# A new opening for a two-block transformer kernel, and its forget-gate logits as split fp32r matmuls

## The chip, the core and the metric

The kernel runs on one core of a Trainium2 chip. The metric is the device time of one execution in microseconds (us); less is better.

## What is computed

Two transformer blocks are applied to one sequence of 256 tokens of width 2048, in fp32. Only the start of the first block is touched by the change:

```
xn = rms_norm(x, norm_mix_g)                  # x: 256 x 2048
proj = xn @ w_in                              # w_in: 2048 x 12296
xa, xpool, xsc, qkv, f_logit, gate_logits = split(proj, ...)
...                                           # xa, xpool, xsc, qkv feed four branches
log_f = log_sigmoid(f_logit + forget_b)       # f_logit: 256 x 8
cum = cumsum(log_f, axis=tokens)              # used in the attention branch
```

The normalization is x * g * rsqrt(mean(x*x) + eps). The kernel multiplies by the gain g (`g_mix`) before the matmul and by the rsqrt factor (`rstd`) after it.

## The kernel before

**Layout.** Activations are held transposed: 16 tiles of 128 channels x 256 tokens. A number is kept as a high part and a low part, both of the type fp32r. `act_a[:, k, 0:S]` is the high part of tile k and `act_a[:, k, S:2*S]` the low part (S = 256).

**Units and pieces.** The weight matrices are read as pieces of 512 rows x 256 columns (512 KB). A unit is 256 output columns, in most phases four pieces (`ppu` = 4, s = 0 to 3). A piece is brought by a transfer that SyncE issues into one of four places of `raw` (L547), copied to fp32r by ScalarE (`w_high`, L879), and the difference is taken by VectorE (`w_low`, L1216). TensorE then does eight pairs of matmuls per piece: high weights by high and low activations in one matmul of 512 columns (L580), and low weights by high activations in one of 256 columns (L582). Semaphores: `raw_full[slot]` (transfer landed), `high_ready`, `split_done` (piece n is split; SyncE waits on it before it refills the place, TensorE before it uses the piece), `w_used` (TensorE has used the piece; ScalarE waits on it before it overwrites `w_high`).

**End of a unit (epilogue).** ScalarE copies the low half of the sums from PSUM (`bcopy`, L893), VectorE adds (`summ`, L1241, semaphore `summed`) and multiplies by `rstd` (L1248). There are two PSUM banks for units, so TensorE starts unit n only when unit n-2 is in `summ`. On ScalarE and VectorE the order is written out: the pieces of the next unit are put ahead of the epilogue of this one (`skewed`).

**Opening.** SyncE issues x as four transfers of four tiles, then all parameter columns (`par`, 249.5 KB), the constants (`common`), and then pieces as their places come free. ScalarE waits for `par`, and for each two tiles of x it makes their squares (`sqt`, L982) and high parts (L984); after every four tiles it casts one piece of the first unit. VectorE makes the low parts (L1343) and w_low of that piece. GpSimd (POOL) adds the squares into `sqacc` (L1657), two tiles at a time, and then starts its own transfers of small operands (L1736 to L1743), among them `w_f`, the eight columns of the forget gate. TensorE works through unit 0 of `proj_a`, piece by piece, then sums the squares over the partitions with a matrix of ones (`ssq`, L615 and L616), and goes on with the other nine units of `proj_a`. From the sum come `rms` (ScalarE, L971) and `rstd` (VectorE, L1332).

**Forget-gate logits.** After the ten units of `proj_a` TensorE computes the logits with fp32 matmuls, 16 tiles by two halves:

```
for k in range(KT):
    for half in range(2):
        last = nc.tensor.matmul(pm[0:HEADS, 0, 0:S], w_f[:, k, :],
                                act_a[:, k, half * S:half * S + S].bitcast(F32), ...)     # L628
```

VectorE takes them from PSUM (L1384, L1385), ScalarE applies abs, exp and ln (L1003 to L1005), VectorE the scan (L1390). Meanwhile TensorE goes on with `proj_b`, three pieces, then the small matmuls of the first branch step (L642, L643, L648). All later phases follow in the same manner.

Of the kernel before, what the change touches and what calls it, by code (L numbers as in the profile page):

```python
# [18 lines left out]
F32 = mybir.dt.float32  # L19
# [5 lines left out]
P = 128  # L25
S = 256
# [92 lines left out]
def plan():  # L119

    ph = [Phase("proj", 10, 2, 4, name="proj_a"), Phase("proj", 6, 2, 4, name="proj_b")]
    for step, q in (("gates", 0), ("gates", 1), ("mix", 0), ("mix", 1),
# [43 lines left out]
def piece_no(ph, i, j, s):  # L166

    return i * (ph.U * ph.ppu) + (ph.piece0 + j * ph.ppu + s)

# [28 lines left out]
def build(nc, A, out):  # L198
# [4 lines left out]
    with ExitStack() as ctx:  # L203
# [22 lines left out]
        rms_buf = sb("rms", [P, S])  # L226
        stat = sb("stat", [P, 84])
        ps = ctx.enter_context(nc.psum_tensor("ps_gemm", [P, 2, 2, 2 * S], F32))
        pm = ctx.enter_context(nc.psum_tensor("ps_small", [P, 4, 2 * S], F32))
# [21 lines left out]
        def pcol(name, i=0):  # L251
# [22 lines left out]
            sem("in_" + n) for n in ("params", "common", "consts1", "w_f", "selectors", "consts2", "p", "resid"))  # L274
        in_x = [sem(f"in_x{b}") for b in range(4)]
        stored = sem("stored")
# [6 lines left out]
        zeroed, bd_zeroed = sem("zeroed"), sem("bd_zeroed")  # L283
        y_high, y_done = sem("y_high"), sem("y_done")
        f_logits, f_biased, f_log, cum_ready, cumt_ps, cumt_ready = (
            sem(n) for n in ("f_logits", "f_biased", "f_log", "cum_ready", "cumt_ps", "cumt_ready"))
# [30 lines left out]
        def source(ph, i, j, s):  # L317
# [3 lines left out]
            k0, kn = 4 * s, 4  # L321
            if n == "proj_a":
                w, c = "w_in", u * 256
            elif n == "proj_b":
                w, c = "w_in", u * 256 + 2560
# [31 lines left out]
        def slot(ph, j, s):  # L357
            return (j * ph.ppu + s) % RING

# [111 lines left out]
        def dst_tile(ph, i, j):  # L471

            q, n, u = ph.quarter, ph.name, i * ph.U + j
            if n == "proj_b":
# [84 lines left out]
        def _(pe):  # L559
# [4 lines left out]

            def piece(ph, x_in, need, i, j, s):

# [6 lines left out]
                pe.wait_ge(split_done, piece_no(ph, i, j, s) + 1 + RING)  # L573
                for k in range(kn):
                    x = x_in(i, j, 4 * s + k)
                    first = s == 0 and k == 0
# [40 lines left out]


            pe.wait_ge(in_common, 16)
# [244 lines left out]
        def _(act):  # L864
# [5 lines left out]
            def piece(ph, i, j, s):  # L870
# [4 lines left out]
                body_rounds = ph.U * ph.ppu // RING  # L875
                rnd = i * body_rounds + (ph.piece0 + j * ph.ppu + s) // RING + 1
                act.wait_ge(raw_full[at], rnd * 16)
# [96 lines left out]
            eps_t = stat[:, 64:65]  # L974

            act.wait_ge(in_par, 16)

            for b in range(8):
                act.wait_ge(in_x[b // 2], 16)
                if b >= 2:  # L980
                    act.wait_ge(sq0_added, b - 1)
                nc.scalar.activation(sqt[:, b % 2], tiles(G, 2 * b, 2), ACT.Square).then_inc(sq0_ready, 1)  # L982
                for t in range(2):
                    last = nc.scalar.activation(act_a[:, 2 * b + t, 0:S], G[:, 2 * b + t, :], ACT.Copy,  # L984
                                                scale=pcol("g_mix", 2 * b + t))
                last.then_inc(hi0, 1)
                if b % 2:
                    piece(BY["proj_a"], 0, 0, b // 2)
            act.wait_ge(zeroed, 1)
# [215 lines left out]
        def _(dve):  # L1205
# [21 lines left out]
            def epilogue(ph, i, j):  # L1227
# [14 lines left out]
                if k in ("proj", "gate", "up", "upconv"):  # L1242
                    dve.wait_ge(summed, n + 1 + 2)
                    r2 = rstd[:].unsqueeze(1).to_broadcast([P, 2, S])
                    if k == "proj":
                        dst = proj_tiles(ph, t0)
                        dve.wait_ge(epi_done, n + 2)
                        nc.vector.tensor_tensor(dst, s2, r2, ALU.mult).then_inc(epi_done, 1)  # L1248
                        return
# [87 lines left out]
            nc.vector.memset(stat[:, 64:65], EPS).then_inc(zeroed, 1)  # L1337
            dve.wait_ge(in_par, 16)
            for b in range(8):
                dve.wait_ge(hi0, b + 1)  # L1340
                for t in range(2):
                    k = 2 * b + t
                    last = nc.vector.scalar_tensor_tensor(out=act_a[:, k, S:2 * S], in0=G[:, k, :],  # L1343
                                                          scalar=pcol("g_mix", k), in1=act_a[:, k, 0:S].bitcast(F32),
                                                          op0=ALU.mult, op1=ALU.subtract)
                last.then_inc(lo0, 1)
                if b % 2:
                    piece(BY["proj_a"], 0, 0, b // 2)

# [15 lines left out]

            pend = skewed(dve, None, BY["proj_a"], pieces, epilogue, True, once=lambda: recip(0))
            ended = []
# [280 lines left out]
        def _(pool):  # L1648
# [191 lines left out]
```

## Time and profile before

| | |
|---|---|
| median of 3 runs | 3088.48 us (3086.43 to 3089.05) |
| the profiled execution's own time | 3071.16 us |
| its span | 3069.3 us |
| mean granted TensorE clock | 0.988 |
| TensorE (PE) busy | 2967.5 us, 97% |
| VectorE (DVE) busy | 1973.4 us, 64% |
| ScalarE (ACT) busy | 1551.1 us, 51% |
| GpSimd (POOL) busy | 257.8 us, 8% |

Times in rows of the trace are counted from the start of the span. An engine's busy time is the time in which at least one of its instructions ran. PEld is the load of stationary operands, which overlaps matmuls. The idle time before an instruction is put down to what released it last.

### The profile page before, as it was taken

The numbers are of one execution on the slowest core, as the hardware profiler recorded it, in microseconds if no ns is written. First come the engines' busy times: TensorE is split into PE (matmuls) and PEld (weight loads), VectorE is DVE, ScalarE is ACT, GpSimd is POOL, SyncE is SP. The second block draws the span as 40 slices with busy tenths as digits, with TensorE's granted clock in tenths as the row PEclk, the third lists the DMA queues.
The fourth block names the chain that finished last, engine by engine and source line by source line (L and its number), as shares of the span: only waits on it lengthen the run. The fifth ranks groups of instructions, "written<-read, shape, count | busy, mean of one in ns | idle before, by whom it ended". The sixth has DMA issues, their size and how long they took to land. (4 is left out here: it accounts for less than half of the span.)

```text
span 3069.3 us, 48743 instructions
## 1 busy us (share of the span) xinstructions
PE 2967.5 (97%) x16830; PEld 2571.2 (84%) x16830; DVE 1973.4 (64%) x2245; ACT 1551.1 (51%) x1953; POOL 257.8 (8%) x217
## 2 busy tenths in 40 slices
PE   7999999999999999999999998999799999999979
PEld 6788888888888888888888887878588888888867
DVE  6486676656665656556656655665777567657664
ACT  5485654454544444444544455444466455545544
POOL 3010011102101010000200000001300000010131
PEclk9999999999999999999999999999899999999989
DMA  7555557665666666665665544546366666565545
GB/s 215 158 165 165 165 167 217 181 178 171 192 192 192 189 188 191 190 187 180 197 191 172 170 148 141 185 151 190 107 187 185 186 190 189 187 185 185 173 134 165
DMA packets 544861, 544.78 MB, mean 177 GB/s; under 512 B 17032, under 2 KB 543880, under 8 KB 544752
## 3 DMA queue, kind: packets, MB, share of 16 engines
q1 hardware_dynamic: 543200, 539.42, 57.7%
q0 software_dynamic: 1552, 3.97, 0.4%
q8 instruction: 60, 0.98, 0.1%
q14 instruction: 49, 0.40, 0.0%
HBM read 541.23 MB, written 2.10 MB: 177 GB/s over the span
## 5 line engine op out<-in xcount | busy, mean ns | idle before, releaser
L1216 DVE TENSOR_TENSOR w_low<-raw,w_high 128x1024 fp32r<-128x1024 f32 x1024 | 1276.3, 1260 | 857.1 <-ACT w_high L879 852.6
L580 PE MATMUL ps_gemm<-act_a,w_high 128*128 128x512 f32 x4640 | 1643.1, 399 | 60.5 <-DVE w_low L1216 39.2
L879 ACT CAST w_high<-raw 128x1024 fp32r<-128x1024 f32 x1024 | 1056.6, 1045 | 961.7 <-PE ps_gemm L582 925.4
L582 PE MATMUL ps_gemm<-act_a,w_low 128*128 128x256 f32 x4640 | 1303.8, 281 | 0.0
L580 PE MATMUL ps_gemm<-act_b,w_high 128*128 128x512 f32 x3520 | 1240.6, 397 | 14.9 <-DVE w_low L1216 5.7
L580 PEld LDWEIGHTS ps_gemm<-act_a,w_high 128*128 128x128 f32 x4640 | 876.9, 189 | 276.6 <-issue 59.5
L582 PE MATMUL ps_gemm<-act_b,w_low 128*128 128x256 f32 x3520 | 986.9, 280 | 0.0
L582 PEld LDWEIGHTS ps_gemm<-act_a,w_low 128*128 128x128 f32 x4640 | 882.6, 190 | 0.2
L580 PEld LDWEIGHTS ps_gemm<-act_b,w_high 128*128 128x128 f32 x3520 | 663.3, 188 | 170.6 <-issue 10.6
L582 PEld LDWEIGHTS ps_gemm<-act_b,w_low 128*128 128x128 f32 x3520 | 667.8, 190 | 0.2
L893 ACT COPY bcopy<-ps_gemm 128x512 f32<-128x512 f32 x300 | 173.6, 579 | 88.1 <-PE ps_gemm L582 88.0
L1241 DVE TENSOR_TENSOR summ<-ps_gemm,bcopy 128x512 f32<-128x512 f32 x276 | 188.8, 684 | 28.1 <-ACT bcopy L893 27.3
L1689 POOL TENSOR_TENSOR proj<-proj,summ 128x512 f32 x32 | 41.4, 1292 | 1016.3 <-DVE summ L1241 1016.3
L1304 DVE SCALAR_TENSOR_TENSOR gates<-summ,params,gates 128x254 f32<-128x254 f32 (+1 forms) x176 | 77.3, 480 | 17.7 <-ACT gates L946 10.7
L1250 DVE TENSOR_TENSOR summ<-summ,rstd 128x512 f32<-128x512 f32 x124 | 85.8, 692 | 4.3
L1675 POOL TENSOR_TENSOR proj<-proj,summ 128x512 f32 x32 | 46.5, 1455 | 400.2 <-DVE summ L1290 400.2
L1657 POOL TENSOR_TENSOR sqacc<-sqacc,sqt 128x512 f32<-128x512 f32 x48 | 67.8, 1413 | 126.4 <-ACT sqt L964 114.3
L912 ACT CAST act_a<-summ 128x512 f32 (+1 forms) x32 | 19.9, 622 | 96.9 <-DVE summ L1263 96.9
L946 ACT ACTIVATE gates<-summ,params 128x256 f32<-128x256 f32 x88 | 48.2, 595 | 21.0 <-DVE summ L1250 19.0
L1257 DVE SCALAR_TENSOR_TENSOR act_b<-proj,params,act_b (+1 forms) x32 | 26.6, 873 | 49.8 <-ACT act_b L905 49.8
L899 ACT ACTIVATE gates<-summ 128x512 f32<-128x512 f32 (+1 forms) x40 | 25.3, 632 | 63.1 <-DVE summ L1250 63.0
L1225 DVE TENSOR_TENSOR act_a<-summ,act_a 128x512 f32 (+1 forms) x32 | 22.2, 693 | 32.5 <-ACT act_a L912 32.5
(239 smaller groups left out, 911.0 us busy)
## 6 DMA issues: line engine op xcount, KB each, us to landing
raw<-in_w_in SPq DMA_DIRECT2D x352, 512.0 KB, 4.2
raw<-in_w_up SPq DMA_DIRECT2D x176, 512.0 KB, 3.6
raw<-in_w_mlp_up SPq DMA_DIRECT2D x128, 512.0 KB, 3.9
raw<-in_w_mlp_down SPq DMA_DIRECT2D x128, 512.0 KB, 4.2
raw<-in_w_down SPq DMA_DIRECT2D x88, 512.0 KB, 4.4
raw<-in_w_out SPq DMA_DIRECT2D x64, 512.0 KB, 4.6
raw<-in_w_branch SPq DMA_DIRECT2D x32, 512.0 KB, 4.0
raw<-in_w_ple_gate SPq DMA_DIRECT2D x32, 512.0 KB, 4.4
```

The lines of the kernel that those rows point to most:

```text
L580: nc.tensor.matmul(ps[:, g, t, :], wh[:, at, o:o + P], x, start=first, stop=False, skip_group_check=True)
L582: last = nc.tensor.matmul(ps[:, g, t, 0:S], wl[:, at, o:o + P], high(x), start=False, stop=final, skip_group_check=True)
L879: nc.scalar.copy(wh[:, at, 0:kn * S], raw[:, at, 0:kn * S]).then_inc(high_ready, 1)
L893: nc.scalar.copy(bcopy[:, g], ps[:, g, :, S:2 * S]).then_inc(b_copied, 1)
L946: last = nc.scalar.activation(G[:, 28 + 2 * j + t, :], summ[:, g, t], ACT.Identity, scale=pcol("conv_w2", c0 + t + 176), bias=pcol("conv_b ...
L1216: nc.vector.tensor_tensor(wl[:, at, 0:kn * S], raw[:, at, 0:kn * S], wh[:, at, 0:kn * S].bitcast(F32), ALU.subtract).then_inc(split_done, 1)
L1241: nc.vector.tensor_tensor(s2, A_half, bcopy[:, g], ALU.add).then_inc(summed, 1)
L1250: nc.vector.tensor_tensor(s2, s2, r2, ALU.mult).then_inc(scaled, 1)
L1304: last = nc.vector.scalar_tensor_tensor(out=y[:, t, sh:S], in0=summ[:, g, t, 0:S - sh], scalar=pcol("conv_w2", c0 + t + 88 * tap), in1=y[: ...
L1657: nc.gpsimd.tensor_tensor(sqacc[:], sqacc[:], sqt[:, g], ALU.add).then_inc(inc, 1)
L1675: nc.gpsimd.tensor_tensor(d, d, s2, ALU.add).then_inc(merged if split else epi_done, 1)
L1689: nc.gpsimd.tensor_tensor(d, d, s2, ALU.add).then_inc(epi_done, 1)
```

## The change

1. **Phases.** The first two units of `proj_a` become a phase `proj_0`; `proj_a` keeps eight. In `proj_0` the pieces are numbered 2s + j, so the two units j = 0, 1 take turns: both use a quarter of x (four tiles) before the next quarter is needed.
2. **Transfers.** The order of SyncE is now: the 16 columns of `g_mix` (`in_gain`), piece (unit 0, s = 0), x tiles 0-1, x tiles 2-3, piece (1, 0), then for s = 1, 2, 3 four tiles of x and the two pieces of that s. `common` and the rest of `par` go ahead of the last two pieces. A piece waits on `split_done` as before.
3. **ScalarE and VectorE.** They wait for `in_gain` in place of `par`; the semaphores `hi0` and `lo0` count single tiles. ScalarE squares four tiles in one instruction, after the second piece of a quarter, into G[16 + 4s], so it no longer waits for GpSimd. GpSimd still adds two tiles at a time, into `sqacc`.
4. **TensorE.** It waits for `lo0` tile by tile within a piece, does `ssq` after both units, and waits for `in_common` only there. `rms` and the epilogues of the two units stand between the pieces of `proj_a` unit 0.
5. **Logits.** ScalarE copies `w_f` to fp32r and VectorE takes the difference, both after `proj_a` on their queues. TensorE then does 48 fp32r matmuls in place of 32 fp32 ones. The product of the two low parts is left out.

```diff
-    ph = [Phase("proj", 10, 2, 4, name="proj_a"), Phase("proj", 6, 2, 4, name="proj_b")]
+    ph = [Phase("proj", 2, 2, 4, name="proj_0"), Phase("proj", 8, 2, 4, name="proj_a"),
+          Phase("proj", 6, 2, 4, name="proj_b")]
...
-            for b in range(4):
-                sp.dma_start(tiles(G, 4 * b, 4), x_v[:, 4 * b:4 * b + 4, :]).then_inc(in_x[b], 16)
-            sp.dma_start(par[:], A["params"]).then_inc(in_par, 16)
-            sp.dma_start(common[:], A["common"]).then_inc(in_common, 16)
-            for ph in PH:
+            sp.dma_start(par[:, 0:ng], A["params"][:, 0:ng]).then_inc(in_gain, 16)
...
+            first_piece(0, 0)
+            x_chunk(0, 0, 2)
+            x_chunk(1, 2, 2)
+            first_piece(1, 0)
+            for s in range(1, 4):
+                x_chunk(s + 1, 4 * s, 4)
+                if s == 3:
+                    sp.dma_start(common[:], A["common"]).then_inc(in_common, 16)
+                    sp.dma_start(par[:, ng:NPAR], A["params"][:, ng:NPAR]).then_inc(in_par, 16)
+                for j in range(2):
+                    first_piece(j, s)
+            for ph in PH[1:]:
...
+            def need_x(s, j, k):
+                if j == 0:
+                    pe.wait_ge(lo0, 4 * s + k + 1)
+            for s in range(4):
+                for j in range(2):
+                    piece(p0, from_buf(act_a), None, 0, j, s, need_x)
             pe.wait_ge(in_common, 16)
-            def need_x(i, j, s):
-                pe.wait_ge(lo0, 2 * (s + 1))
-            units(BY["proj_a"], from_buf(act_a), need_x, lambda: ssq(0, sq0_added, 8))
-            pe.wait_ge(in_wf, 16)
+            ssq(0, sq0_added, 8)
+            units(BY["proj_a"], from_buf(act_a))
+            pe.wait_ge(wf_low, 1)
             for k in range(KT):
-                for half in range(2):
-                    last = nc.tensor.matmul(pm[0:HEADS, 0, 0:S], w_f[:, k, :],
-                                            act_a[:, k, half * S:half * S + S].bitcast(F32),
-                                            start=(k == 0 and half == 0), stop=(k == KT - 1 and half == 1))
+                nc.tensor.matmul(pm[0:HEADS, 0, 0:S], wf_s[:, 0, k, :], act_a[:, k, 0:S], start=(k == 0), stop=False)
+                nc.tensor.matmul(pm[0:HEADS, 0, 0:S], wf_s[:, 0, k, :], act_a[:, k, S:2 * S], start=False,
+                                 stop=False)
+                last = nc.tensor.matmul(pm[0:HEADS, 0, 0:S], wf_s[:, 1, k, :], act_a[:, k, 0:S], start=False,
+                                        stop=(k == KT - 1))
...
-            for b in range(8):
-                act.wait_ge(in_x[b // 2], 16)
-                if b >= 2:
-                    act.wait_ge(sq0_added, b - 1)
-                nc.scalar.activation(sqt[:, b % 2], tiles(G, 2 * b, 2), ACT.Square).then_inc(sq0_ready, 1)
-                for t in range(2):
-                    last = nc.scalar.activation(act_a[:, 2 * b + t, 0:S], G[:, 2 * b + t, :], ACT.Copy,
-                                                scale=pcol("g_mix", 2 * b + t))
-                last.then_inc(hi0, 1)
-                if b % 2:
-                    piece(BY["proj_a"], 0, 0, b // 2)
+            piece(p0, 0, 0, 0)
+            for s in range(4):
+                if s:
+                    piece(p0, 0, 0, s)
+                for k in range(4 * s, 4 * s + 4):
+                    if k in (0, 2, 4, 8, 12):
+                        act.wait_ge(in_x[(0, 2, 4, 8, 12).index(k)], 16)
+                    nc.scalar.activation(act_a[:, k, 0:S], G[:, k, :], ACT.Copy,
+                                         scale=pcol("g_mix", k)).then_inc(hi0, 1)
+                piece(p0, 0, 1, s)
+                nc.scalar.activation(tiles(G, 16 + 4 * s, 4), tiles(G, 4 * s, 4), ACT.Square).then_inc(sq0_ready, 1)
             act.wait_ge(zeroed, 1)
-            pend = None
-            pend = skewed(act, None, BY["proj_a"], pieces, epilogue, True, once=lambda: rms(0))
+            act.wait_ge(in_par, 16)
+            piece(pa, 0, 0, 0)
+            piece(pa, 0, 0, 1)
+            epilogue(p0, 0, 0)
+            rms(0)
+            piece(pa, 0, 0, 2)
+            piece(pa, 0, 0, 3)
+            pend = skewed(act, lambda: epilogue(p0, 0, 1), pa, pieces, epilogue, True)
+            act.wait_ge(in_wf, 16)
+            nc.scalar.copy(wf_s[:, 0], w_f).then_inc(wf_high, 1)
...
+            dve.wait_ge(wf_high, 1)
+            nc.vector.tensor_tensor(wf_s[:, 1], w_f, wf_s[:, 0].bitcast(F32), ALU.subtract).then_inc(wf_low, 1)
...
-                add_square(b % 2, sq0_ready, b + 1, sq0_added)
+                pool.wait_ge(sq0_ready, b // 2 + 1)
+                nc.gpsimd.tensor_tensor(sqacc[:], sqacc[:], tiles(G, 16 + 2 * b, 2), ALU.add).then_inc(sq0_added, 1)
```

VectorE's opening is reordered as ScalarE's is: piece (0, s), four low parts, piece (1, s), and then the pieces of `proj_a` unit 0 with the epilogue of the first unit (which has `recip(0)` in it, between its add and its multiply) after the second of them.

## Rows read from the trace of the kernel before

**Rows 1.** The page, part 1: busy time and share of each engine.

```profile
PE 2967.5 (97%) x16830; PEld 2571.2 (84%) x16830; DVE 1973.4 (64%) x2245; ACT 1551.1 (51%) x1953; POOL 257.8 (8%) x217
```

**Rows 2.** Busy time by stretch: opening, logits. Ahead of GB/s: granted clock, DMA share.

```profile
0.00:17.26 17.26, 0.00 (x0) 0.03 (x1) 5.41 (x7) 8.18 (x15) 5.78 (x9) 1.00 0.81 265
17.26:33.39 16.13, 13.00 (x63) 10.88 (x64) 15.46 (x17) 9.55 (x17) 14.81 (x18) 1.00 0.51 125
33.39:45.30 11.91, 11.91 (x69) 10.45 (x68) 7.44 (x7) 7.28 (x8) 5.74 (x11) 1.00 0.89 257
...
134.30:148.20 13.90, 13.90 (x65) 5.69 (x64) 3.60 (x8) 4.61 (x7) 0.75 (x2) 1.00 0.30 82
```

**Rows 3.** Waits from 0 to 60 us: in total, times, longest, all in us.

```profile
PE ps_gemm L580 <- DVE w_low L1216: 20.4, 3, 17.3
...
ACT w_high L879 <- DMA raw<-in_w_in: 12.4, 5, 7.5
```

**Rows 4.** Timeline of ScalarE: start, duration, work, idle before it.

```profile
4.73 1.28 ACT L982 ACT_TABLE_LOAD   x1 [4.73 <-DMA gates<-in_x_t]
10.37 0.63 ACT L982 ACTIVATE sqt<-gates 128x512 f32<-128x512 f32 x1 [4.36 <-DMA params<-in_params]
...
22.98 0.89 ACT L984 ACTIVATE act_a<-gates,params 128x256 fp32r<-128x256 f32 x2
23.78 1.98 ACT L879 CAST w_high<-raw 128x1024 fp32r<-128x1024 f32 x2
```

**Rows 5.** Waits from 125 to 185 us.

```profile
DVE proj L1384 <- PE ps_small L628: 8.7, 1, 8.7
...
PE ps_small L648 <- DVE gates L1420: 0.7, 1, 0.7
```

**Rows 6.** Timeline of TensorE in the opening.

```profile
18.04 0.63 PE L580 MATMUL ps_gemm<-act_a,w_high 128*128 128x512 f32 x1
...
18.68 0.63 PE L580 MATMUL ps_gemm<-act_a,w_high 128*128 128x512 f32 x1
...
23.08 0.47 PE L580 MATMUL ps_gemm<-act_a,w_high 128*128 128x512 f32 x1 [1.38 <-DVE w_low L1216]
...
28.54 0.28 PE L582 MATMUL ps_gemm<-act_a,w_low 128*128 128x256 f32 x1
28.65 0.39 PE L580 MATMUL ps_gemm<-act_a,w_high 128*128 128x512 f32 x1
...
33.51 0.59 PE L615 MATMUL ps_small<-sqacc,common 128*128 128x256 f32 x2
...
34.18 0.58 PE L580 MATMUL ps_gemm<-act_a,w_high 128*128 128x512 f32 x1
```

**Rows 7.** The transfers of x: their issues on SyncE's queue, and issue to landing.

```profile
0.82 2.10 SPq L536 DMA_DIRECT2D gates<-in_x_t  x4
...
DMA to landing us min/median/max: 3.8/5.6/7.2
```

**Rows 8.** Timeline of VectorE in the opening.

```profile
14.82 2.29 DVE L1216 TENSOR_TENSOR w_low<-raw,w_high 128x1024 fp32r<-128x1024 f32 x1
17.04 4.76 DVE L1343 SCALAR_TENSOR_TENSOR act_a<-gates,params,act_a 128x256 fp32r<-128x256 f32 x4
...
27.66 1.66 DVE L1343 SCALAR_TENSOR_TENSOR act_a<-gates,params,act_a 128x256 fp32r<-128x256 f32 x4
...
29.24 3.48 DVE L1216 TENSOR_TENSOR w_low<-raw,w_high 128x1024 fp32r<-128x1024 f32 x3
...
40.24 1.75 DVE L1332 RECIPROCAL rstd<-rms 128x256 f32<-128x256 f32 x1 [0.56 <-ACT rms L971]
```

**Rows 9.** Timeline of GpSimd in the opening.

```profile
14.72 6.40 POOL L1657 TENSOR_TENSOR sqacc<-sqacc,sqt 128x512 f32<-128x512 f32 x4 [0.90 <-ACT sqt L982]
```

**Rows 10.** The instructions of L628, the logits: durations in ns, first and last start.

```profile
L628 PE MATMUL ps_small<-act_a,small_ops x64: 378/379/382, 134.3 to 147.9; 128*8 128x256 f32 x64
```

**Rows 11.** The adds of squares up to 40 us: durations in ns, first and last start.

```profile
L1657 POOL TENSOR_TENSOR sqacc<-sqacc,sqt x8: 1266/1352/2191, 11.2 to 24.2; 128x512 f32<-128x512 f32 x8
```

More of the change, by code:

```diff
@@ L166, in piece_no @@
 def piece_no(ph, i, j, s):
+    if ph.name == "proj_0":
+        return 2 * s + j
     return i * (ph.U * ph.ppu) + (ph.piece0 + j * ph.ppu + s)
@@ L227, in build @@
         stat = sb("stat", [P, 84])
+        wf_s = sb("w_f_split", [P, 2, KT, HEADS], F32R)
         ps = ctx.enter_context(nc.psum_tensor("ps_gemm", [P, 2, 2, 2 * S], F32))
@@ L274, in build @@
             sem("in_" + n) for n in ("params", "common", "consts1", "w_f", "selectors", "consts2", "p", "resid"))
-        in_x = [sem(f"in_x{b}") for b in range(4)]
+        in_x = [sem(f"in_x{b}") for b in range(5)]
+        in_gain = sem("in_gain")
         stored = sem("stored")
@@ L284, in build @@
         y_high, y_done = sem("y_high"), sem("y_done")
+        wf_high, wf_low = sem("wf_high"), sem("wf_low")
         f_logits, f_biased, f_log, cum_ready, cumt_ps, cumt_ready = (
@@ L321, in source @@
             k0, kn = 4 * s, 4
-            if n == "proj_a":
+            if n == "proj_0":
                 w, c = "w_in", u * 256
+            elif n == "proj_a":
+                w, c = "w_in", u * 256 + 512
             elif n == "proj_b":
@@ L357, in slot @@
         def slot(ph, j, s):
-            return (j * ph.ppu + s) % RING
+            return (2 * s + j if ph.name == "proj_0" else j * ph.ppu + s) % RING
         def over(eng, body, start, end):
@@ L473, in dst_tile @@
             q, n, u = ph.quarter, ph.name, i * ph.U + j
+            if n == "proj_a":
+                return u * 2 + 4
             if n == "proj_b":
@@ L534, in _, with first_piece, x_chunk @@
             sp.sem_inc(split_done, RING)
-            for b in range(4):
-                sp.dma_start(tiles(G, 4 * b, 4), x_v[:, 4 * b:4 * b + 4, :]).then_inc(in_x[b], 16)
-            sp.dma_start(par[:], A["params"]).then_inc(in_par, 16)
-            sp.dma_start(common[:], A["common"]).then_inc(in_common, 16)
-            for ph in PH:
+            ng = COL["g_mlp"]
+            sp.dma_start(par[:, 0:ng], A["params"][:, 0:ng]).then_inc(in_gain, 16)
+            def first_piece(j, s):
+                ph = BY["proj_0"]
+                n, at = piece_no(ph, 0, j, s), slot(ph, j, s)
+                sp.wait_ge(split_done, n + 1)
+                sp.dma_start(raw[:, at, :].rearrange("p (t n) -> p t n", t=4),
+                             source(ph, 0, j, s)).then_inc(raw_full[at], 16)
+            def x_chunk(c, k, n):
+                sp.dma_start(tiles(G, k, n), x_v[:, k:k + n, :]).then_inc(in_x[c], 16)
+            first_piece(0, 0)
[10 more added lines that the diff above has]
+            for ph in PH[1:]:
                 def body(i, ph=ph):
@@ L563, in high, with piece @@
                 return t[:, 0:S]
-            def piece(ph, x_in, need, i, j, s):
+            def piece(ph, x_in, need, i, j, s, need_tile=None):
                 n, g, at = unit_no(ph, i, j), bank(ph, j), slot(ph, j, s)
@@ L574, in piece @@
                 for k in range(kn):
+                    if need_tile:
+                        need_tile(s, j, k)
                     x = x_in(i, j, 4 * s + k)
@@ L875, in piece @@
                 body_rounds = ph.U * ph.ppu // RING
-                rnd = i * body_rounds + (ph.piece0 + j * ph.ppu + s) // RING + 1
+                rnd = i * body_rounds + piece_no(ph, 0, j, s) // RING + 1
                 act.wait_ge(raw_full[at], rnd * 16)
@@ L974, in _ @@
             eps_t = stat[:, 64:65]
-            act.wait_ge(in_par, 16)
-            for b in range(8):
-                act.wait_ge(in_x[b // 2], 16)
-                if b >= 2:
-                    act.wait_ge(sq0_added, b - 1)
-                nc.scalar.activation(sqt[:, b % 2], tiles(G, 2 * b, 2), ACT.Square).then_inc(sq0_ready, 1)
-                for t in range(2):
-                    last = nc.scalar.activation(act_a[:, 2 * b + t, 0:S], G[:, 2 * b + t, :], ACT.Copy,
-                                                scale=pcol("g_mix", 2 * b + t))
-                last.then_inc(hi0, 1)
-                if b % 2:
-                    piece(BY["proj_a"], 0, 0, b // 2)
-            act.wait_ge(zeroed, 1)
-            pend = None
-            pend = skewed(act, None, BY["proj_a"], pieces, epilogue, True, once=lambda: rms(0))
+            act.wait_ge(in_gain, 16)
+            p0, pa = BY["proj_0"], BY["proj_a"]
+            piece(p0, 0, 0, 0)
[9 more added lines that the diff above has]
+                nc.scalar.activation(tiles(G, 16 + 4 * s, 4), tiles(G, 4 * s, 4), ACT.Square).then_inc(sq0_ready, 1)
+            act.wait_ge(zeroed, 1)
+            act.wait_ge(in_par, 16)
+            piece(pa, 0, 0, 0)
[7 more added lines that the diff above has]
+            nc.scalar.copy(wf_s[:, 0], w_f).then_inc(wf_high, 1)
             ended = []
@@ L1246, in epilogue @@
                         dst = proj_tiles(ph, t0)
+                        if ph.name == "proj_0" and j == 0:
+                            recip(0)
                         dve.wait_ge(epi_done, n + 2)
@@ L1337, in _ @@
             nc.vector.memset(stat[:, 64:65], EPS).then_inc(zeroed, 1)
[L1338 to L1348, printed above, removed]
+            dve.wait_ge(in_gain, 16)
+            p0, pa = BY["proj_0"], BY["proj_a"]
+            piece(p0, 0, 0, 0)
+            for s in range(4):
+                if s:
+                    piece(p0, 0, 0, s)
+                for k in range(4 * s, 4 * s + 4):
+                    dve.wait_ge(hi0, k + 1)
+                    nc.vector.scalar_tensor_tensor(out=act_a[:, k, S:2 * S], in0=G[:, k, :],
+                                                   scalar=pcol("g_mix", k), in1=act_a[:, k, 0:S].bitcast(F32),
+                                                   op0=ALU.mult, op1=ALU.subtract).then_inc(lo0, 1)
+                piece(p0, 0, 1, s)
             def one(pend, ph, started=False, once=None):
@@ L1364, in phases @@
                 return pend
-            pend = skewed(dve, None, BY["proj_a"], pieces, epilogue, True, once=lambda: recip(0))
+            dve.wait_ge(in_par, 16)
+            piece(pa, 0, 0, 0)
+            piece(pa, 0, 0, 1)
+            epilogue(p0, 0, 0)
+            piece(pa, 0, 0, 2)
+            piece(pa, 0, 0, 3)
+            pend = skewed(dve, lambda: epilogue(p0, 0, 1), pa, pieces, epilogue, True)
+            dve.wait_ge(wf_high, 1)
+            nc.vector.tensor_tensor(wf_s[:, 1], w_f, wf_s[:, 0].bitcast(F32), ALU.subtract).then_inc(wf_low, 1)
             ended = []
```

1 line of the change is left out of this document (added).

## The prediction

> **What bounds the kernel now.** I read the page first, for the engine that is always busy; then the busy time by stretch, to find where it isn't; then the waits there and the timelines of single engines. TensorE is busy 97% of the span [rows 1], VectorE 64%. So time taken off TensorE's path early on moves all that follows, unless another engine can't keep up there. In the opening TensorE has nothing to do for 17.26 us and idles another 3.1 us up to the end of unit 0 at 33.4 [rows 2]; the waits name the first piece's w_low for 17.3 us of it [rows 3]. Behind that stand the transfers: ScalarE loads its table at 4.73, when the first x is there, and starts to work at 10.37, when `par` has landed behind all of x [rows 4]. From there to 45.3, and in the logits block of 13.9 us, TensorE is 100% busy [rows 2]. Behind the block it stops once for 0.7 us, for VectorE's L1420 [rows 5].
>
> **The opening, step by step.** I compare when TensorE has done two units and `ssq`. Before: `ssq` takes 0.7 (33.51 to the next unit's first matmul at 34.18), and a unit is 32 pairs. A pair takes 0.345 (the 256 columns start at 28.54, the next 512 at 28.65; 0.115 for the 256 ones, 0.23 for the 512), so a unit takes 11.05, and the mark is at 34.18 + 11.05 = 45.2 [rows 6].
>
> *Transfers.* The first one of 512 KB lands 3.8 us after its issue [rows 7]. Between 4.73 and 10.37, 3 x 512 + 249.5 KB land [rows 4], that is 1.6 us per 512 KB. With the gain's issue (0.5, a quarter of the 2.1 that the four of x take) [rows 7] ahead, piece 0 is there at 5.2, the two halves of the first x at 6.0 and 6.8, piece 1 at 8.4, the second x at 10.0, pieces 2 and 3 at 11.6 and 13.2, x at 14.8, pieces 4 and 5 at 16.4 and 18.0, the last x at 19.6, `common` and the rest of `par` at 20.8, pieces 6 and 7 at 22.4 and 24.0. The waits on `split_done` (piece 4 needs piece 0 split) are met earlier.
>
> *ScalarE.* A cast takes 0.99, a high part 0.44 [rows 4], a square of two tiles 0.63, so one of four between 1.05 (a cast of that size) and 1.26; I take 1.05. A quarter costs 2 x 0.99 + 4 x 0.44 + 1.05 = 4.8, under the 5.5 that TensorE needs for it (16 pairs). It starts with piece 0 at 5.2, or up to 1.3 later if the table load waits for that transfer; I take 6.0. The first w_high is there at 7.0.
>
> *VectorE.* w_low takes 1.16 and a low part 0.42 undisturbed (3.48/3, 1.66/4) [rows 8]. First w_low 8.2, first low part 8.6, so TensorE starts at about 8.8 in place of 17.26. But with GpSimd adding, the same w_low took 2.29 and four low parts 4.76 [rows 8, 9]. From 14.82 to the three w_low at 29.24 VectorE did three w_low and twelve low parts without a wait: 3 x 1.16 + 12 x 0.42 = 8.5 of work in 14.4 us, beside six adds. That is 1.0 lost per add. In the new order it has 8 x 1.16 + 16 x 0.42 = 16.0 of work; the first quarter's two adds fall partly into its one wait (some 1.2 us for piece 2), so six collide. Its last w_low ends at 7.0 + 16.0 + 1.2 + 6 x 1.0 = 30.2.
>
> *TensorE.* The first 2.7 us go at half the pace (0.64 per pair at 18.04 and 18.68, rows of a stretch whose granted clock is given as 1.00) [rows 2, 6]; that costs 1.3, as before. Alone it would take 8.8 + 64 x 0.345 + 1.3 = 32.2. VectorE's last piece gives 30.2 + 8 x 0.345 = 33.0. With `ssq`, 0.7, the mark is at 33.7; a late start of ScalarE would shift it by 0.5 more. I take 34.2: **11.0 us gained**. Bounds: TensorE alone, 32.9, gains 12.3. All eight adds colliding at the 1.6 that they took in the worst stretch (6.40/4) [rows 9] are 12.8 in place of 6.0: the mark at 40.5, 4.7 gained.
>
> *What is late next.* Unit 2 needs unit 0 in `summ`. ScalarE and VectorE put two pieces ahead of it, all possible before the mark: TensorE is still in piece 7 (2.8) and `ssq` (0.7) while the copy and the add run (under 1.0 each by the forms of their size, w_low at 1.16 being twice as large). `rms`, the reciprocal, the multiply and one w_low then stand ahead of piece 10: 0.5 + 1.75 + 0.7 + 1.16 = 4.1 [rows 8] (the first as a high part of the same size, the third 0.6 of w_low's 1.16, for half its elements), against two pieces of TensorE, 5.5. This holds with 1.4 to spare; a table load of 1.28 behind `ssq` [rows 4] would just use it up. GpSimd's small transfers start later than before, behind the last add; beside them ScalarE waited up to 7.5 for a piece [rows 3] without a stop of TensorE, which had pieces in hand. The same holds here, with some 2 us to spare.
>
> **The logits.** 64 instructions from 134.3 to 147.9 are 0.2125 each; with the last one's rest the block takes 13.6 [rows 10]. An fp32r matmul of 256 columns costs 0.115 in the pairs [rows 6]: 48 x 0.115 = 5.5. **8.1 us gained.** Bounds: half of the 512-column time, 0.23/2, is the same 0.115, and without any cost beside the columns (half of 0.2125) 0.106, which gives 8.5; if eight-column weights went at the fp32 pace, 48 x 0.2125 = 10.2 and 3.4 gained. The added copy and subtraction of `w_f` (128 columns, well under 0.5 each) lie during the last unit of `proj_a`, which lasts 11 us; without that cover they would cost 0.6. Would the gain be lost behind? VectorE waits 8.7 us for the logits [rows 5]. With the block 8.1 shorter it still waits 0.6. So its chain to L1420 starts from the end of the logits as before, and the stop of 0.7 stays 0.7.
>
> *A rule weighed.* The Trainium skill, "SBUF — State Buffer", section on two separate sides, says that VectorE with two SBUF inputs and a GpSimd operation that reads SBUF exclude each other for whole instructions. The w_low of 2.29 agrees: it began 0.1 after an add and took 1.13 longer than undisturbed [rows 8, 9]. Were the exclusion complete, the mark would be later, as the first rival has it.
>
> **Sum.** 11.0 + 8.1 = 19.1. The profiled execution goes from 3071.2 to 3052.1. The median of the runs is 17.3 above it, 0.6%, which no row explains; I carry the difference over: 3088.5 - 19.1 = **3069.4**.
>
> **The rivals.**
> - *GpSimd and VectorE block each other fully.* Each of seven adds that meet VectorE costs it the shortest add, 1.27 [rows 11], 8.9 in place of 6.0. The mark is at 37.1, the gain 8.1 + 8.1 = 16.2: 3072.3. For it: the 2.29 and the 4.76 [rows 8]. Against it: the mean of 1.0 over six adds.
> - *A new wait for transfers.* TensorE's ring is emptier after the opening, as it takes pieces as soon as they are split, and GpSimd's 22 small transfers fall on it. If pieces come 7.5 late [rows 3] and only half is covered, the gain is 19.1 - 3.8 or less: 3073 to 3077. Against it: 33.4 to 45.3 shows no idle time under the same load [rows 2].
> - *The logits block doesn't shorten as said*: 3.4 of 8.1, or the stop at L648 grows by what VectorE is late. Total 14.4: 3074.1.
> - *The other side: TensorE's clock.* It begins with 0.64 a pair, twice 0.345 nearly, the lower of its levels (1.2 of 2.4 GHz), and rises after steady work. If the new start, fed tile by tile, kept it at the low level, each pair would cost 0.295 more. The gain of 19.1 is used up at 65 pairs beyond the four of before, that is just over the two units; from 86 pairs on it is slower by over 0.2%. Held through a third unit: 92 x 0.295 = 27.1, so 3096.5. Against it: a stop of 1.38 us did not bring the low level back (0.47 at 23.08, no longer 0.63) [rows 6].
>
> **How the numbers follow.** My forecast 0.67 (its own range 3066 to 3072); full blocking 0.12; transfers 0.08; logits 0.07; clock 0.04; a gain of over 23 us, for instance as the runs don't share the profile's offset, 0.02. The 80% range leaves out the clock and the ends of the transfer case: 3065 to 3077. A measurement here tells 0.2% (6 us) from no change. Faster: all but the clock case and a scrap of the transfer one, 0.94; same 0.03; slower 0.03.
>
> **What would show it.** TensorE's first matmul near 9 us, with hardly any idle time up to the mark near 34; VectorE busy without a stop from some 12 to 30, w_low at 2.3 where adds run; the table load of `rms` ahead of the end of `ssq`; the logits as 48 instructions in 5.5 us; a wait of VectorE before L1384 of about half a us, and the stop before L648 still 0.7. I would be wrong if TensorE stood before w_low for over 3 us after its start, if its pace stayed at 0.64, or if later stretches idled more than before. By order and count nothing behind 160 us changes.

## The result, and the profile after

The changed kernel takes 3070.16 us (median of 7 runs, 3060.61 to 3075.15), the kernel before 3089.05 (7 runs on the same chip, 3086.43 to 3101.74). The ratio is 0.9938, with a 95% interval of 0.9916 to 0.9959: faster, by 12.7 to 26 us; the medians differ by 18.9, and 19.1 was forecast. The profiled execution tells less than that: its span is 3064.9 us against 3069.3, only 4.4 less. Experiment 8 shows where the rest went.

The waits of the changed kernel from 0 to 60 us; L611 is the first matmul of a pair (L580 before), L1263 is w_low, L1395 the low parts of x:

```profile
DVE w_low L1263 <- ACT w_high L918: 13.2, 9, 7.3
PE ps_gemm L611 <- DVE act_a L1395: 10.3, 2, 10.1
...
ACT w_high L918 <- DMA raw<-in_w_in: 10.2, 7, 3.2
...
ACT L918 <- DMA raw<-in_w_in: 5.9, 1, 5.9
...
DVE rstd L1381 <- ACT rms L1010: 1.9, 1, 1.9
```

Its busy time by stretch (columns as in [rows 2]):

```profile
8.80:20.00 11.20, 9.90 (x48) 8.48 (x48) 10.54 (x12) 11.07 (x19) 6.41 (x4) 1.00 1.10 349
20.00:30.00 10.00, 9.36 (x52) 7.87 (x52) 10.00 (x10) 6.56 (x9) 6.39 (x4) 1.00 0.65 185
30.00:40.00 10.00, 9.98 (x56) 8.45 (x55) 8.03 (x10) 4.33 (x5) 9.69 (x18) 1.00 0.83 205
```

TensorE starts at 10.10 in place of 17.26 and then idles 0.66 us up to 40 (0.64 of it from 20 to 30), where it idled 3.1 before [rows 2]. VectorE is busy 10.00 of 10 from 20 to 30. The mark, where two units and the sum of squares are done, is the row at 36.14 below; it was 45.2 [rows 6]. TensorE's timeline:

```profile
10.10 0.77 PE L611 MATMUL ps_gemm<-act_a,w_high 128*128 128x512 f32 x1 [10.10 <-DVE act_a L1395]
...
12.16 0.63 PE L611 MATMUL ps_gemm<-act_a,w_high 128*128 128x512 f32 x1
...
12.80 0.53 PE L611 MATMUL ps_gemm<-act_a,w_high 128*128 128x512 f32 x1
...
30.42 0.50 PE L611 MATMUL ps_gemm<-act_a,w_high 128*128 128x512 f32 x1
...
35.46 0.59 PE L646 MATMUL ps_small<-sqacc,common 128*128 128x256 f32 x2
35.89 0.59 PE L647 MATMUL ps_small<-sqacc,common 128*128 128x256 f32 x2
36.14 0.58 PE L611 MATMUL ps_gemm<-act_a,w_high 128*128 128x512 f32 x1
...
126.77 0.28 PE L665 MATMUL ps_small<-act_a,w_f_split 128*8 128x256 f32 x1
...
132.24 0.28 PE L668 MATMUL ps_small<-act_a,w_f_split 128*8 128x256 f32 x1
132.35 0.40 PE L611 MATMUL ps_gemm<-act_a,w_high 128*128 128x512 f32 x1
```

So the opening gained 45.2 - 36.1 = 9.1 us. The logits now last 132.35 - 126.77 = 5.58 us. Before they began at 134.31 and the next matmul at 148.22, 13.91 later (134.3 in [rows 10]): 8.3 gained. Together 17.4.

Not all of that arrives behind the logits. The product at L648 of the kernel before starts at 158.56, the same product of the changed kernel at 142.79, which is 15.8 earlier. Most of the other 1.6 us went between the mark and the logits: the same 514 recorded matmuls took 90.6 us in place of 89.0, with TensorE busy throughout and a granted clock of 1.00 in both. Experiment 8 shows that this is not the change's doing either.

ScalarE and VectorE at the start, where the forecast was off:

```profile
5.88 1.28 ACT L918 ACT_TABLE_LOAD   x1 [5.88 <-DMA raw<-in_w_in]
7.18 1.04 ACT L918 CAST w_high<-raw 128x1024 fp32r<-128x1024 f32 x1
...
33.45 1.28 ACT L1010 ACT_TABLE_LOAD   x1
36.52 0.47 ACT L1010 ACTIVATE rms<-ps_small,stat 128x256 f32<-128x256 f32 x1 [1.79 <-PE ps_small L647]
```

```profile
9.47 1.67 DVE L1395 SCALAR_TENSOR_TENSOR act_a<-gates,params,act_a 128x256 fp32r<-128x256 f32 x4
...
14.43 3.75 DVE L1395 SCALAR_TENSOR_TENSOR act_a<-gates,params,act_a 128x256 fp32r<-128x256 f32 x4
...
27.42 3.74 DVE L1395 SCALAR_TENSOR_TENSOR act_a<-gates,params,act_a 128x256 fp32r<-128x256 f32 x4
31.08 3.48 DVE L1263 TENSOR_TENSOR w_low<-raw,w_high 128x1024 fp32r<-128x1024 f32 x3
```

The first table load stands behind the landing of piece 0 and ahead of its cast; that of `rms` is done before the sum of squares. Four low parts take 1.67 in the first quarter, and 3.74 in later ones, beside GpSimd's adds. The first of the three w_low at 31.08 is that of piece 7, done at about 32.2; TensorE comes to that piece at 32.64, and is done at 35.46. TensorE's last wait is the one before 30.42, for the second low part of the last quarter (done at 30.4 beside an add). From there on its pairs follow each other without a stop, so it is VectorE's low parts in the last quarter that place the mark, and not its last w_low.

### The profile page after: what moved, and what is told of

Read it like the earlier page. It is cut to its first block and busy times, and to the rows that moved or that the text cites. A ratio compares the mean times of both kernels' runs of the same rounds, so it can differ in the third digit from the quotient of the medians.

```text
span 3064.9 us, 48670 instructions
## 1 busy us (share of the span) xinstructions
PE 2972.4 (97%) x16814; PEld 2572.1 (84%) x16814; DVE 1972.3 (64%) x2246; ACT 1551.4 (51%) x1950; POOL 257.0 (8%) x217
## 5 line engine op out<-in xcount | busy, mean ns | idle before, releaser
L1263 DVE TENSOR_TENSOR w_low<-raw,w_high 128x1024 fp32r<-128x1024 f32 x1024 | 1275.3, 1259 | 869.8 <-ACT w_high L918 865.6
L611 PE MATMUL ps_gemm<-act_a,w_high 128*128 128x512 f32 x4640 | 1650.4, 400 | 50.6 <-DVE w_low L1263 19.1
L611 PE MATMUL ps_gemm<-act_b,w_high 128*128 128x512 f32 x3520 | 1247.3, 399 | 15.0 <-DVE w_low L1263 5.7
L611 PEld LDWEIGHTS ps_gemm<-act_a,w_high 128*128 128x128 f32 x4640 | 878.2, 189 | 270.7 <-issue 46.4
L611 PEld LDWEIGHTS ps_gemm<-act_b,w_high 128*128 128x128 f32 x3520 | 663.7, 189 | 177.4 <-issue 10.7
L1715 POOL TENSOR_TENSOR sqacc<-sqacc,sqt 128x512 f32<-128x512 f32 x40 | 55.2, 1380 | 116.2 <-ACT sqt L1003 115.9
```

The source lines that it names most:

```text
L611: nc.tensor.matmul(ps[:, g, t, :], wh[:, at, o:o + P], x, start=first, stop=False, skip_group_check=True)
L1263: nc.vector.tensor_tensor(wl[:, at, 0:kn * S], raw[:, at, 0:kn * S], wh[:, at, 0:kn * S].bitcast(F32), ALU.subtract).then_inc(split_done, 1)
L1715: nc.gpsimd.tensor_tensor(sqacc[:], sqacc[:], sqt[:, g], ALU.add).then_inc(inc, 1)
```

## The experiments

Four places of TensorE in one profile of each kernel, in us: its first matmul, the mark, the first matmul of the logits, and the first of the product at L648 of the kernel before (the two kernels with the adds later put the sum elsewhere, so they have no mark). The last column is the number of matmuls that the profile shows from 60 to 100 us, where TensorE is always busy:

| kernel | first matmul | mark | logits begin | L648 | matmuls, 60 to 100 us |
|---|---|---|---|---|---|
| before | 17.26 | 45.2 | 134.3 | 158.6 | 233 |
| changed | 10.1 | 36.1 | 126.8 | 142.8 | 229 |
| opening only | 9.9 | 35.85 | 126.6 | 150.8 | 229 |
| logits only | 17.1 | 45.1 | 136.0 | 151.9 | 229 |
| table load early | 8.6 | 35.2 | 124.2 | 140.1 | 233 |
| one add | 9.7 | 34.7 | 125.4 | 141.4 | 229 |
| gain columns first | 14.8 | 43.85 | 132.9 | 157.2 | 233 |
| unit by unit | 9.8 | 41.15 | 130.1 | 146.0 | 233 |
| adds later | 9.2 | – | 125.3 | 141.2 | 228 |
| changed, again | 10.1 | 36.1 | 126.7 | 142.8 | 229 |
| changed, warm | 10.1 | 36.2 | 125.1 | 141.1 | 232 |
| adds later, warm | 8.9 | – | 124.0 | 140.0 | 229 |

(For the two kernels that keep the old opening's order, the mark is worked out from the end of their first unit and sum: 34.06 or 32.80, plus 11.05.) From the mark to the logits every profile with 232 or 233 takes 88.9 to 89.1 us, and every one with 229 takes 90.6 to 90.9. So the columns behind the mark can be compared only between kernels with the same last column.

**1 and 2. The halves apart.** The changed kernel with the logits of before, and the kernel before with the new logits:

```diff
-            pe.wait_ge(wf_low, 1)
+            pe.wait_ge(in_wf, 16)
             for k in range(KT):
...
+                for half in range(2):
+                    last = nc.tensor.matmul(pm[0:HEADS, 0, 0:S], w_f[:, k, :],
```
```diff
-            pe.wait_ge(in_wf, 16)
+            pe.wait_ge(wf_low, 1)
             for k in range(KT):
...
+                nc.tensor.matmul(pm[0:HEADS, 0, 0:S], wf_s[:, 0, k, :], act_a[:, k, 0:S], start=(k == 0), stop=False)
```

> The changed kernel with the fp32 logits of before. Theory (two separate gains on TensorE's path that add up): the mark after two units and the sum of squares stays at 36.1 us as in the changed kernel (45.2 before), the logits block lasts 13.9 us again, and the time is 9 us under before, ratio 0.997. Rival (the gain is all from the logits, as the opening's is lost later): ratio 1.000, with the first small matmul L648 of before no more than 2 us earlier than 158.6. Rival (nearly all is the opening): ratio 0.994.

> The kernel before with the logits as 48 fp32r matmuls. Theory: the mark stays at 45.2 us, the block takes 5.6 in place of 13.9, L648 comes 8.3 earlier at 150.3, VectorE waits about 0.3 us for the logits in place of 8.7; ratio 0.9973. Rival (VectorE's chain behind the logits takes the gain back): TensorE stops before L648 for over 3 us in place of 0.7, and the ratio is over 0.999.

The opening alone gives 3061.9 us, ratio 0.9945 (0.9921 to 0.9969); the logits alone 3069.81, ratio 0.9965 (0.9942 to 0.9988); the kernel before on that chip had 3075.99 (3066.28 to 3093.23). Both are faster by themselves. The time of the opening alone doesn't decide between theory and rival: 0.9945 is the 0.994 of the rival, and the theory's 0.997 lies just outside its interval. But the intervals are some 15 us wide, as wide as the gains themselves (14.1 and 6.2 us), so the places in the profile say more. The opening alone has its mark at 35.85, and its logits last from 126.58 to 140.49, 13.91 again; its product of L648 is 8.0 behind the changed kernel's, so the opening is not nearly all. The logits alone last from 136.01 to 141.46, 5.45. Their product of L648 was expected at 150.3 and came at 151.9: by the table, that is about the 1.7 us between the profiles with 233 and those with 229. The waits in the logits-only kernel, where the gain could have been taken back:

```profile
ACT gates L1008 <- DVE proj L1392: 1.6, 1, 1.6
...
PE ps_small L651 <- DVE gates L1427: 0.9, 1, 0.9
...
DVE proj L1391 <- PE ps_small L632: 0.2, 1, 0.2
```

VectorE waits 0.2 us for the logits in place of 8.7 [rows 5], and TensorE's stop behind them is 0.9 in place of 0.7. The block could lose 8.3 us with no loss behind it, and hardly any more: the next microsecond taken from it would be VectorE's wait turned round. That last is argued, not tried.

**3. The table load early.**

```diff
+            nc.scalar.preload_act_table(ACT.Square)
             act.wait_ge(in_gain, 16)
```

> The changed kernel with ScalarE's table load asked for ahead of its first waits. Theory (the first table load of 1.28 us stands behind the landing of piece 0 and ahead of its cast): the table load comes before 4 us, the first cast at 5.9 in place of 7.2, TensorE's first matmul at 8.8 in place of 10.1, and the mark at 34.9 to 35.5 in place of 36.1 since VectorE with GpSimd beside it then limits more. Rival (the table load waits for something else, or the engine is not ready): it stays at 5.9 and nothing moves.

Time 3059.03 us. (Experiments 3 to 6 and 9 have one run each, which is too few for an interval; what they show is in their profiles.) ScalarE's timeline:

```profile
0.74 1.28 ACT L1015 ACT_TABLE_LOAD   x1 [0.74 <-PEq L1894]
5.72 1.04 ACT L918 CAST w_high<-raw 128x1024 fp32r<-128x1024 f32 x1 [3.70 <-DMA raw<-in_w_in]
```

TensorE starts at 8.65, which is the 8.8 of the prediction, and the mark is at 35.2: of 1.45 us gained at the start 0.9 is left at the mark. The logits' 124.2 contains another 1.7 us that is not the table load's (last column of the table).

**4. One add.**

```diff
-                nc.gpsimd.tensor_tensor(sqacc[:], sqacc[:], tiles(G, 16 + 2 * b, 2), ALU.add).then_inc(sq0_added, 1)
+                if b == 0:
+                    nc.gpsimd.tensor_tensor(sqacc[:], sqacc[:], tiles(G, 16 + 2 * b, 2), ALU.add).then_inc(sq0_added, 1)
+                else:
+                    pool.sem_inc(sq0_added, 1)
```

> The changed kernel in which GpSimd adds only the first two tiles of squares; the other seven adds are left out, so the sum of squares is too small. Theory (each add costs VectorE about one us): w_low takes 1.2 and a low part 0.42 throughout, VectorE waits for ScalarE between pieces, its last w_low of the two units ends at about 28 in place of 32.3, and TensorE's stops in 20 to 30 us (0.64) vanish, so the mark is at 35.5 in place of 36.1, no more, since TensorE started at 10.1. Rival (the low parts are slow because of the transfers into their memory): four low parts still take 3.7 us.

VectorE in the last quarter:

```profile
24.72 1.67 DVE L1395 SCALAR_TENSOR_TENSOR act_a<-gates,params,act_a 128x256 fp32r<-128x256 f32 x4
26.30 1.22 DVE L1263 TENSOR_TENSOR w_low<-raw,w_high 128x1024 fp32r<-128x1024 f32 x1
28.09 1.23 DVE L1263 TENSOR_TENSOR w_low<-raw,w_high 128x1024 fp32r<-128x1024 f32 x1 [0.56 <-ACT w_high L918]
```

Low parts at 1.67 everywhere: the 3.74 is GpSimd's, not the transfers'. The w_low of piece 7 (at 26.30) is done at 27.5 in place of 32.2. TensorE doesn't idle between its start and the mark, which is at 34.72, 1.4 earlier (0.6 was expected); 0.4 of that is an earlier start. The time is 3055.67 us. The Trainium skill ("SBUF — State Buffer", two separate sides) has such pairs of operations exclude each other for whole instructions. The runs agree that GpSimd's adds hold up the low parts, with 3.74 beside 1.67. That is 1.0 lost per add, less than the shortest add of this profile, 1.34, so no run here shows that a whole add is always lost.

**5. The gain columns first, nothing else** (on the kernel before).

```diff
+            sp.dma_start(par[:, 0:ng], A["params"][:, 0:ng]).then_inc(in_gain, 16)
...
-            sp.dma_start(par[:], A["params"]).then_inc(in_par, 16)
+            sp.dma_start(par[:, ng:NPAR], A["params"][:, ng:NPAR]).then_inc(in_par, 16)
```

> The kernel before, with only the 16 gain columns ahead of x and the rest of the parameters behind it (what the change does to par, and nothing else). Theory (the order of piece 0 behind all of x is what holds TensorE, not the parameters alone): ScalarE starts squares at about 6.5 in place of 10.4, but piece 0 still lands near 12.5, so its cast is at 12.7 to 13.2 in place of 13.02, w_low ends near 14.5 (16 to 17 before), and TensorE starts at 14.7 to 15.5 in place of 17.26. Rival (par was the cause alone): TensorE starts at 11 or earlier.

```profile
6.71 0.63 ACT L985 ACTIVATE sqt<-gates 128x512 f32<-128x512 f32 x1
...
12.38 1.04 ACT L882 CAST w_high<-raw 128x1024 fp32r<-128x1024 f32 x1 [2.92 <-DMA raw<-in_w_in]
```

The time is 3072.06 us. ScalarE starts 3.7 us earlier, then waits 2.92 for piece 0 behind all of x, and TensorE starts at 14.8. Its first unit and sum end at 32.80 in place of 34.18 [rows 6]: 1.4 gained. Of the 7.2 us by which TensorE starts earlier in the changed kernel, 2.4 come from the parameters. The other 4.7 come from the rest of the change, and piece 0 alone moves by more than that: its cast starts at 7.18 in place of 12.38.

**6. Unit by unit.**

```diff
-        return 2 * s + j
+        return 4 * j + s
...
-            for s in range(4):
-                for j in range(2):
+            for j in range(2):
+                for s in range(4):
```

The same order stands in SyncE's, ScalarE's and VectorE's loops.

> The changed kernel, but the four pieces of unit 0 first and then those of unit 1, in transfers, on all engines and in the numbering. Theory (sharing each quarter of x gives TensorE 5.6 us of work per quarter, against 4.8 that VectorE needs for one piece, four low parts and two adds): TensorE starts at 10.1 but stops about 2 us before each of the next three quarters, and the mark is at 39.5 to 41 in place of 36.1. Rival (the early start is all that counts, the sharing is worth nothing): the mark is under 37.

Its waits from 0 to 60 us, then its busy time by stretch:

```profile
PE ps_gemm L611 <- DVE act_a L1396: 14.0, 8, 9.8
```

```profile
10.00:20.00 10.00, 8.20 (x32) 6.11 (x32) 9.18 (x10) 9.83 (x18) 8.32 (x5) 1.00 1.02 325
20.00:30.00 10.00, 7.58 (x37) 5.71 (x38) 10.00 (x12) 4.47 (x7) 9.45 (x13) 1.00 0.53 123
```

The time is 3061.61 us. The start is nearly the same, but TensorE waits seven more times for low parts, 4.2 us in all, and the mark is at 41.15. So 5.0 of the opening's 9.1 us are the sharing of quarters by two units, and 4.1 all the rest, the early start first of all.

**7. The adds later.** With the early table load; six of the eight adds wait for the eighth piece to be split, and the sum of squares comes one unit later.

```diff
-            ssq(0, sq0_added, 8)
-            units(BY["proj_a"], from_buf(act_a))
+            units(BY["proj_a"], from_buf(act_a), None, lambda: ssq(0, sq0_added, 8))
...
                 pool.wait_ge(sq0_ready, b // 2 + 1)
+                if b == 2:
+                    pool.wait_ge(split_done, 8 + RING)
```

> The changed kernel with the table load first, the adds of the last six halves of squares held back until the eighth piece is split, and the sum of squares one unit later (behind the first unit of proj_a). Theory (table load and GpSimd's adds cost the opening what the prediction lacked): TensorE starts at 8.6 to 8.8, four low parts of the later quarters take 1.67, and TensorE has its first 64 pairs done at 32.0 to 32.5 in place of 35.46, 3 us earlier; the logits start 3 us earlier at the same pace of pairs. Ratio to before 0.9935 to 0.9925, not to be told from the changed kernel's in three rounds. Rival (the adds only move the wait: the reciprocal behind the later sum holds the pieces of the second unit): TensorE stops for over 2 us between 43 and 60.

3056.53 us (10 runs, 3046.53 to 3064.53), ratio 0.9938 (0.9909 to 0.9968). TensorE isn't idle once from 9.2 to 100, so the rival falls, but the later sum starts at 45.27, which is some 34.2 for the two units (a unit takes 11.1 here), 1.3 earlier than the changed kernel's 35.46, not 3. The rest went at the start: TensorE began at 9.22 for the 8.6 to 8.8 expected, and it kept the low pace until 14.9 us, 5.7 us long. That is nine pairs, against four in the changed kernel (until the pair at 12.80) and four before [rows 6].

**8. The changed kernel once more.**

> The changed kernel once more, on this chip. Theory (pairs go at two paces, 455 or 463 matmuls in 80 us, over stretches of hundreds of us that have nothing to do with the change): the mark is at 36.1 and L648's first matmul at 142 to 143 again, but the number of matmuls in the stretches 800 to 900 up to 1300 to 1400 may be 567 or 579 whatever it was. Rival (the slower pace there is an effect of the change): 567 in all four stretches again, although the kernels with half the change or the early table load had 579.

3057.29 us (10 runs, 3047.14 to 3068.28; before on that chip 3079.59, 3061.52 to 3097.57), ratio 0.9944 (0.9914 to 0.9973). The places up to L648 repeat within 0.1 us, though the low pace at the start lasted five pairs here and four in the first profile. The later places don't repeat. Busy time by stretch, first of the changed kernel's first profile, then of this one:

```profile
900.00:1000.00 100.00, 100.00 (x567) 86.72 (x566) 55.50 (x50) 43.02 (x47) 9.03 (x7) 1.00 0.59 180
```

```profile
900.00:1000.00 100.00, 100.00 (x579) 87.47 (x578) 57.30 (x53) 42.97 (x47) 9.07 (x7) 1.00 0.61 188
```

And the casts of the four `mlp_up` phases in the two:

```profile
L951 ACT CAST act_a<-summ x32: 620/621/623, 804.3 to 1424.6; 128x512 f32 x22, 128x512 fp32r<-128x512 f32 x10
```

```profile
L951 ACT CAST act_a<-summ x32: 621/622/624, 804.1 to 1412.7; 128x512 f32 x22, 128x512 fp32r<-128x512 f32 x10
```

With TensorE busy throughout and the granted clock at 1.00, the same program took 620.3 us once and 608.6 the other time for the same work. The chip can't be the reason: both paces stand in each of the two profiles, 579 from 2500 to 2600 us in the first and 568 in this one. The kernel before had the fast pace there, 820.4 to 1429.0, also 608.6. So the 16.1 us that the changed kernel was ahead at 804 shrank to 4.4 at 1425, and that isn't the change's doing. The 229 or 233 matmuls from 60 to 100 us are the same two paces: kernels with the new opening had either. What decides between them no run shows.

**9 and 10. A warm start.** Ten fp32 matmuls of zeros ahead of the first piece, in the changed kernel and in the one with the adds later.

```diff
+            nc.vector.memset(sqt[:, 0], 0.0).then_inc(warm, 1)
...
+            pe.wait_ge(warm, 1)
+            for _ in range(10):
+                nc.tensor.matmul(pm[:, 2, 0:S], sqt[:, 0, 0, 0:P], sqt[:, 0, 1, :], start=True, stop=True)
```

> The changed kernel, with ten fp32 matmuls of zeros of 256 columns on TensorE ahead of its first piece, into an unused bank. Theory (the slow first 3.8 to 5.7 us, 0.64 a pair, come from TensorE having stood still, and cost 1.7 to 2.6): the matmuls of zeros start near 2 and end by 9, the first pair of the first piece already takes 0.35. In the changed kernel VectorE then holds TensorE more, so the mark moves from 36.1 by less than 1. Rival (the low pace belongs to the first real matmuls whatever ran before): pairs of 0.64 after 10.1 as before.

> The kernel with the early table load and the later adds, and the ten matmuls of zeros. Theory (with VectorE free, TensorE alone sets the pace, so the warm start counts in full): first real matmul at 8.7 to 9.2, pairs of 0.345 from there on, the two units done near 31.5, the later sum of squares at 42.6 in place of 45.3, and the logits 1.3 to 2.6 earlier than 125.3 at the same pace. Ratio to before 0.993. Rival (VectorE or the transfers now hold the second quarter): stops of TensorE of over 1 us between 10 and 30.

The tenth kernel's TensorE:

```profile
1.65 7.52 PE L658 MATMUL ps_small<-sqt 128*128 128x256 f32 x20 [1.65 <-DVE sqt L1389]
8.94 0.47 PE L612 MATMUL ps_gemm<-act_a,w_high 128*128 128x512 f32 x1
9.24 0.28 PE L614 MATMUL ps_gemm<-act_a,w_low 128*128 128x256 f32 x1
9.36 0.39 PE L612 MATMUL ps_gemm<-act_a,w_high 128*128 128x512 f32 x1
```

Both have pairs of 0.35 from the start, so the rival falls. In the changed kernel it gives nothing: TensorE only waits more often, its last wait for a low part ends at 30.45 as before, and the mark is at 36.18. (Its logits at 125.1 in place of 126.8 are the other pace.) With the adds later it counts: the sum starts at 44.00 in place of 45.27, though 42.6 was expected; TensorE stopped once for 0.64 us, at 15.47, under the 1 us of the rival. Time of the ninth 3058.84 (one run); of the tenth 3053.76 (6 runs, 3048.9 to 3055.74), ratio 0.9919 (0.9898 to 0.9941) to the kernel before on that chip, 3076.86. That is the best ratio of all, with the logits at 124.0 in place of 126.7 at the same pace, but its interval and the changed kernel's overlap.

## Why the prediction was right

**The bound.** Right. TensorE's path moved, and no wait ahead of L648 took the gain back. What was lost on the way, 1.6 us, is pace.

**The logits.** Right in size: 8.3 us for 8.1, a matmul of 256 columns at 0.115 (the 48 take 5.58), VectorE's wait left at 0.3 for the forecast 0.6, the stop 0.9 for 0.7. Experiment 2 has the same with the old opening.

**The opening.** The mechanism was right, the size 1.9 us too large: the mark at 36.1 for 34.2. Two terms were mis-sized. The first: "It starts with piece 0 at 5.2, or up to 1.3 later if the table load waits for that transfer; I take 6.0". Piece 0 was there at 5.9, 0.7 late, and the table load did wait, so the cast began at 7.2. Experiment 3 takes the 1.28 away, and TensorE's start goes to 8.65. The second was what the adds cost VectorE. From 8.33 to 32.2 it did 16.0 us of work and waited 0.66, so 7.3 us went to eight adds, 0.9 each, where I had six at 1.0. With seven adds left out (experiment 4) its last piece is done 4.7 us earlier. The price of an add was nearly right, the number was not: all eight fell on VectorE's work, and the wait that was to hide the first two was 0.66 us for the forecast 1.2. So the first rival, full blocking, is nearer to the truth than the forecast put it: its 8.9 was too much, my 6.0 too little, and the mark of 36.1 is nearer its 37.1 than my 34.2, though a part of that is the late start. The path was also a little different: TensorE was held last by a low part, up to 30.42, and not by VectorE's last piece. The low pace at the start was as forecast, 2.7 us; experiment 9 shows that in this kernel it costs the mark nothing.

**What is late next.** Right: the table load of `rms` stood ahead of the sum, the two pieces ahead of the first epilogue held nothing up, and ScalarE's waits for transfers (up to 3.2) reached TensorE nowhere.

**The sum.** 17.4 by the two places, and 15.8 of it at L648, for 19.1. The profiled execution was forecast at 3052.1 us and took 3066.8. That the medians differ by 18.9 is luck within an interval of 12.7 to 26 us. A measurement of this kernel tells less than the 0.2% that the prediction allowed: seven runs against seven leave 0.4% between the ends.

**The other rivals.** The pace did begin low, at 0.64 a pair, but for four pairs as before, and not for the 65 more that would have been needed; transfers and the logits' chain cost nothing.

**The offset of 17.3 us** between profile and median, which I carried over unexplained, was 3.4 in the changed kernel (3070.16 and 3066.8), so it was no constant. It has a likely cause in the two paces of experiment 8. That the longer executions are those with more of the slower pace is argued, since the runs without a profile have no rows.

## What to carry to other kernels

When the bound engine waits at the start, list what it needs for its first piece and issue just that, then let as much work as possible share each arriving part: here sharing was worth more (5.0 us) than all the rest of the new opening, the early start with it (4.1). Ask for the activation table before the first wait. Where GpSimd and VectorE work on SBUF side by side, count each operation of GpSimd as a loss on VectorE (0.9 us for each of eight adds here), also those that seem to fall into a wait; and compare places in two profiles up to the point that the change can reach, as a span can hide 12 us of an unrelated pace.

## What the runs showed of the hardware

- TensorE, 100% busy at a granted clock of 1.00, goes at one of two paces over hundreds of us: 579 or 567 matmuls recorded in 100 us (608.6 or 620.3 us for the same work). The same program shows either, and one execution shows both.
- The low pace at the start (0.64 a pair in place of 0.345, granted clock shown as 1.00) lasted four pairs, 2.7 us, in the kernel before and in the changed one, five in the changed kernel's second profile, and nine, 5.7 us, in experiment 7. After 7 us of matmuls of zeros it is gone, and 1.35 us of idle time behind them don't bring it back (the first real matmul at 10.07 took 0.47).
- Four low parts of VectorE take 1.67 us, and 3.74 beside two adds of GpSimd (experiment 4 against the changed kernel).
- The first table load waited for ScalarE's first transfer (5.88); that of `rms` went ahead of the wait for the sum (33.45, with the sum's last matmul at 35.89).
